# A decoder layer on one core: the second feed-forward stage in two passes of seven block products

## What is computed

```python
def swiglu(h, wg, wu, wd):
    return (jax.nn.silu(h @ wg) * (h @ wu)) @ wd

h = x * (1 + mod[:, 1]) + mod[:, 0]
x = layer_norm(ALPHA*x + 0.5*mod[:, 2]*swiglu(h, ffn1_wg, ffn1_wu, ffn1_wd), ...)
h = x * (1 + mod[:, 4]) + mod[:, 3]
out = mixer(h)                       # attention, then w_out
x = layer_norm(ALPHA*x + mod[:, 5]*out, ...)
h = x * (1 + mod[:, 7]) + mod[:, 6]
x = layer_norm(ALPHA*x + 0.5*mod[:, 8]*swiglu(h, ffn2_wg, ffn2_wu, ffn2_wd), ...)
```

## Time and profile before

| what | value |
|---|---|
| runs | 2271.41, 2273.47, 2273.75 us; median 2273.47 |
| profiled execution, first to last instruction | 2265.1 us |
| median less the profiled span | 8.4 us |
| mean granted TensorE clock, share of full | 0.986 |
| busy share of PE, DVE, ACT, POOL | 95%, 34%, 26%, 27% |

### The profile page before, as it was taken

One profiled execution on the slowest core, in us unless ns is written; L12 is line 12 of the kernel. 1 busy time (PEld: TensorE's weight loads), 2 busy tenths in 40 slices (PEclk: granted clock), 3 DMA queues, 4 the chain that ended last, 5 costly groups with the idle time before them and its releaser, 6 DMA issues.

```text
span 2265.1 us, 33136 instructions
## 1 busy us (share of the span) xinstructions
PE 2161.6 (95%) x13244; PEld 1976.8 (87%) x13244; DVE 778.9 (34%) x1709; ACT 580.7 (26%) x1071; POOL 614.4 (27%) x397
## 2 busy tenths in 40 slices
PE   6799999999999998999979989999999999999997
PEld 2689999999999997998844449899999999999995
DVE  1532122321223229202365652751222211222327
ACT  2311111112111123422265561361111111111114
POOL 1232322223222230124233333132323232323210
PEclk8899999999999999999989999999999999999999
DMA  8372222321321110413242012111111111111002
GB/s 288 131 231 94 84 66 93 112 93 38 112 93 38 47 38 19 148 47 108 101 169 106 1 38 66 38 47 48 56 37 56 37 56 37 56 37 56 28 1 75
DMA packets 168942, 171.36 MB, mean 76 GB/s; under 512 B 14370, under 2 KB 130834, under 8 KB 168324
## 3 DMA queue, kind: packets, MB, share of 16 engines
q1 hardware_dynamic: 168836, 169.84, 23.2%
HBM read 156.91 MB, written 19.20 MB: 78 GB/s over the span
## 4 chain that ended last, share of the span: by engine, by line
PE 87%; DVE 6%; ACT 2%; issue 2%; SPq 2%; DMA 1%; POOL 0%; DVEq 0%; ACTq 0%
PE psum L211 26%; PE psum L213 25%; PE psum L212 25%; PE psum L1086 2%; PE psum L546 2%; PE psum L1145 1%; PE psum L987 1%; DVE NT L694 1%; PE psum L1443 1%; DMA ADA<-in_w_ada 1%; SPq L499 1%; PE psum L644 1%; DVE Y L659 1%; DVE Y L679 1%; PE psum L1136 1%
## 5 line engine op out<-in xcount | busy, mean ns | idle before, releaser
L211 PE MATMUL psum<-Hhi,Whi 128*128 128x344 f32 x2736 | 878.7, 321 | 19.5 <-DVE Hlo L703 10.3
L213 PE MATMUL psum<-Hhi,Wlo 128*128 128x344 f32 x2736 | 875.2, 320 | 0.0
L212 PE MATMUL psum<-Hlo,Whi 128*128 128x344 f32 x2736 | 874.4, 320 | 0.0
L313 POOL TENSOR_TENSOR Wlo<-RAW,Whi 128x1024 fp32r<-128x1024 f32 x158 | 383.2, 2446 | 696.9 <-ACT Whi L309 696.3
L211 PEld LDWEIGHTS psum<-Hhi,Whi 128*128 128x128 f32 x2736 | 515.9, 189 | 29.9 <-issue 23.0
L213 PEld LDWEIGHTS psum<-Hhi,Wlo 128*128 128x128 f32 x2736 | 515.6, 188 | 0.0
L212 PEld LDWEIGHTS psum<-Hlo,Whi 128*128 128x128 f32 x2736 | 514.9, 188 | 0.3
L436 DVE TENSOR_TENSOR GF<-SIL,psum 128x344 f32<-128x344 f32 x132 | 67.6, 512 | 902.7 <-ACT SIL L400 900.1
L443 DVE SCALAR_TENSOR_TENSOR Y<-psum,G,Y 128x344 f32<-128x344 f32 (+1 forms) x528 | 301.2, 573 | 180.5 <-PE psum L213 180.5
L211 PE MATMUL psum<-Ghi,Whi 128*128 128x344 f32 x1056 | 340.2, 322 | 2.4 <-DVE Y L443 2.4
L212 PE MATMUL psum<-Glo,Whi 128*128 128x344 f32 x1056 | 338.0, 320 | 0.0
(11 more groups left out here) (192 smaller groups left out, 1312.0 us busy)
## 6 DMA issues: line engine op xcount, KB each, us to landing
ADA<-in_w_ada SPq DMA_DIRECT2D x38, 1024.0 KB, 9.6
RAW<-in_ffn_wg SPq DMA_DIRECT2D x44, 512.0 KB, 3.8
RAW<-in_ffn_wu SPq DMA_DIRECT2D x44, 512.0 KB, 3.7
RAW<-in_ffn_wd SPq DMA_DIRECT2D x44, 512.0 KB, 3.7
RAW<-in_w_in SPq DMA_DIRECT2D x36, 256.0 KB, 3.2
SK<-in_cache_a_k SPq DMA_DIRECT2D x24, 256.0 KB, 3.5
...
```

The source lines that it names most:

```text
L211: pe.matmul(out, whi, xhi, start=first, stop=False)
L212: pe.matmul(out, whi, xlo, start=False, stop=False)
L213: return pe.matmul(out, wlo, xhi, start=False, stop=last)
L313: pool.tensor_tensor(Wlo[slot][:, :, :], RAW[raw][:, :, :], Whi[slot][:, :, :].bitcast(F32), ALU.subtract).then_inc(W[phase].ready, 1)
```

## The change

The 1032 columns of the second feed-forward stage become four groups of 258 (GQ). A pass works on two groups side by side (pass 0: groups 0 and 1; pass 1: groups 2 and 3), and both passes go over all 11 chunks, so there are 22 chunk-passes and all weights are fetched and split twice. In a chunk-pass the gate and the up product are each a 2x2 block product: 2 tiles of D_FF by 2 halves of D_MODEL, times 2 halves of D_MODEL by 2 groups of columns. Instead of eight block products, seven are made, of sums and differences of blocks (the Winograd form of Strassen's method); each block product is 4 tiles times three matmuls of 258 columns. The sums of weights are made by VectorE (`row_sums`, `row_differences`), those of the inputs once a pass (`column_sums`), and results are combined in PSUM and by ScalarE and VectorE (`part_act`, `add_dve`). The low parts of the blocks stay on GpSimd (`row_lo`), the low parts of the down weights move to VectorE (`drow_lo`). The output projection also works in four groups of 258. The norm of groups 0 and 1 behind the stage, and the store of the first four blocks of 128 tokens, move into pass 1; five blocks are left for the end.

The core of the diff:

```diff
+GQ = T // 4
+NP = 7
...
+        LOWK, HIGHK = slice(0, KT // 2), slice(KT // 2, KT)
+        W_SOURCE = [[PAIR[u][:, 0, LOWK, :], PAIR[u][:, 0, HIGHK, :], S2[u][:, :, :], S1[u][:, :, :],
+                     PAIR[u][:, 1, LOWK, :], PAIR[u][:, 0, HIGHK, :], PAIR[u][:, 1, HIGHK, :]] for u in range(2)]
+        W_SUM = {2: 3, 3: 1, 4: 5, 5: 7}
...
+        def row_sums(dve, r, first=False):
+            for u in range(2):
+                if u == 0 and not first:
+                    dve.wait_ge(r_ready, PR * r - 6)
+                dve.wait_ge(pair_in[u], 32 * r + 32)
+                dve.tensor_tensor(S1[u][:, :, :], PAIR[u][:, 1, LOWK, :], PAIR[u][:, 1, HIGHK, :], ALU.add).then_inc(sums_done, 1)
+            for u in range(2):
+                dve.wait_ge(sums_done, 8 * r + 1 + u)
+                dve.tensor_tensor(S2[u][:, :, :], S1[u][:, :, :], PAIR[u][:, 0, LOWK, :], ALU.subtract).then_inc(sums_done, 1)
...
+        def product_pe(pe, r, n, p, fresh=False, first=False):
+            i, u = n // 2, n % 2
+            a, x = bank[2 * u], bank[2 * u + 1]
+            pe.wait_ge(r_ready, PR * r + n + 1)
...
+            out = (x if i in (1, 3, 5) else a)[:, 0:GQ]
+            whi, wlo = Rhi[n % NP], Rlo[n % NP]
+            for k in range(KT // 2):
+                pe.matmul(out, whi[:, k, :], Thi[i][:, k, :], start=(k == 0 and i in (0, 1, 3)), stop=False, skip_group_check=True)
+                pe.matmul(out, whi[:, k, :], Tlo[i][:, k, :], start=False, stop=False, skip_group_check=True)
+                last = pe.matmul(out, wlo[:, k, :], Thi[i][:, k, :], start=False, stop=(k == KT // 2 - 1), skip_group_check=True)
+            last.then_inc(prod_done, 1)
+        def down_pe2(pe, r, v, first=False):
+            side, d = 1 - v // KT, v % KT
+            if v == 0:
+                pe.wait_ge(dw_ready, 2 * r + 2)
+            if v % KT == 0:
+                pe.wait_ge(g_ready2, 4 * r + 3 + v // KT)
+            if v >= 3:
+                pe.wait_ge(y_evac2, ROWS2 * r + v - 2)
+            elif not first:
+                pe.wait_ge(y_evac2, ROWS2 * r)
+            bk = bank[4 + v % 3][:, 0:GQ]
+            for j in range(2):
+                last = mm3(pe, bk, Whi[4 + j][:, d, :], Wlo[4 + j][:, d, :],
+                           Ghalf[0][:, j, side, :], Ghalf[1][:, j, side, :], j == 0, j == 1)
+            last.then_inc(down_done2, 1)
+        def chunk_pe(pe, r, p, fresh=False, first=False, mean=None, early=None, last=False):
+            for n in range(PR):
+                product_pe(pe, r, n, p, fresh, first)
+                if n == 3 and mean is not None:
+                    for g in mean:
+                        mean_pe(pe, *g)
+                if early is not None and n in (3, 9):
+                    early_turn_pe(pe, early, n // 6)
+            if first:
+                pe.wait_ge(ln_centered, ln[2].n_at(3))
+            for v in range(ROWS2):
+                down_pe2(pe, r, v, first)
+                if last and v == ROWS2 - 2:
+                    mean_pe(pe, ln[3], 3)
...
+        def later_blocks(dve, r):
+            add_dve(dve, r, 1, 0)
+            add_dve(dve, r, 1, 1)
+            gf_dve2(dve, r, 1)
+            for j in range(2):
+                drow_lo(dve, r, j)
+            add_dve(dve, r, 2, 0)
+            add_dve(dve, r, 2, 1)
+            gf_dve2(dve, r, 2)
+            gf_dve2(dve, r, 3)
+        def downs_dve(dve, r, p, more=True, norm=None):
+            for v in range(KT):
+                down_dve2(dve, r, p, v, norm)
+            if more:
+                row_sums(dve, r + 1)
+            elif p:
+                dve.wait_ge(y_evac2, ROWS2 * r + KT)
+                samples_in(dve, ln[3])
+            for v in range(KT, ROWS2):
+                down_dve2(dve, r, p, v, norm)
+        def chunk_dve(dve, r, p, center_at=None, scale_at=None):
+            row_differences(dve, r)
+            if scale_at is not None:
+                scaled(dve, *scale_at)
+            first_blocks(dve, r)
+            if center_at is not None:
+                center(dve, *center_at)
+            later_blocks(dve, r)
+            downs_dve(dve, r, p)
...
+        def chunk_pool(pool, r, more=True):
+            for n in range(NP, PR):
+                row_lo(pool, r, n)
+            g_lo_pool2(pool, r, 0)
+            for b in range(1, 4):
+                g_lo_pool2(pool, r, b)
+            if more:
+                for n in range(NP):
+                    row_lo(pool, r + 1, n)
```

More of the change, by code:

```diff
@@ new lines, in inputs_dve @@
+        def inputs_dve(dve, g):
+            n, p, side = ln[2], g // 2, g % 2
+            own = n.prompt(g)
+            m = own.stop - own.start
+            dve.wait_ge(ln_scaled, n.scaled_at(g, 1))
+            if m < GQ:
+                ts = NQ[side][:, :, m:]
+                step_dve(dve, dve.tensor_tensor(ts, Y[:, :, TP:], A9[:, :, 1:], ALU.mult))
+                dve.tensor_tensor(ts, ts, B9[:, :, 1:], ALU.add)
+            for k in range(KT):
+                last = dve.tensor_scalar(NQ[side][:, k, 0:m], Y[:, k, own], A9[:, k, 0:1], B9[:, k, 0:1], ALU.mult, ALU.add)
+                if side == 0 and k == KT // 2 - 1:
+                    last.then_inc(t_src, 1)
+            last.then_inc(t_src, 1)
@@ new lines, in column_lo, with residual_pool @@
+        def column_lo(dve, p, i):
+            dve.wait_ge(t_hi, NP * p + i + 1)
+            dve.tensor_tensor(Tlo[i][:, :, :], T_SOURCE[i], Thi[i][:, :, :].bitcast(F32), ALU.subtract).then_inc(t_ready, 1)
+        def residual_pool(pool, g):
+            pool.wait_ge(t_src, (2, 3)[g])
+            for k in range(KT):
+                y = Y[:, k, ln[2].cols(g)]
+                last = pool.tensor_scalar(y, y, yv[:, 0, k:k + 1], yv[:, 1, k:k + 1], ALU.mult, ALU.add)
+            last.then_inc(res_done, 1)
@@ L1832, in _ @@
+            chunk_act(act, CH + 2, std_at=(ln[3], 0))
+            input_hi(act, ln[3], 0)
+            for b in range(4):
+                chunk_act(act, CH + 3 + b, early=b)
+            with act.Fori(CH + 7, 2 * CH - 1) as c:
+                chunk_act(act, c)
+            chunk_act(act, 2 * CH - 1, more=False)
+            square(act, ln[3], 3)
             load_sqrt(act)
-            square(act, ln[3], 1)
-            std(act, ln[3], 0)
-            input_hi(act, ln[3], 0)
-            std(act, ln[3], 1)
@@ new lines, in _ @@
+            row_differences(dve, 0)
+            first_blocks(dve, 0)
+            column_lo(dve, 0, 3)
+            last_column_sum(dve, 0)
+            for i in range(4, NP):
+                column_lo(dve, 0, i)
+            later_blocks(dve, 0)
+            center(dve, ln[2], 2)
+            center(dve, ln[2], 3)
+            prep_gate(dve, 8, 0.5)
+            dve.wait_ge(res_done, 2)
+            downs_dve(dve, 0, 0)
+            chunk_dve(dve, 1, 0, scale_at=(ln[2], 2))
+            chunk_dve(dve, 2, 0, scale_at=(ln[2], 3))
@@ new lines, in _ @@
+            inputs_dve(dve, 2)
+            chunk_dve(dve, 3, 0)
+            inputs_dve(dve, 3)
+            chunk_dve(dve, 4, 0)
+            column_sums(dve, 1)
+            with dve.Fori(5, CH - 1) as c:
+                chunk_dve(dve, c, 0)
+            row_differences(dve, CH - 1)
+            first_blocks(dve, CH - 1)
+            column_lo(dve, 1, 0)
+            column_lo(dve, 1, 1)
+            column_lo(dve, 1, 2)
+            add_dve(dve, CH - 1, 1, 0)
+            add_dve(dve, CH - 1, 1, 1)
@@ new lines, in _ @@
+            gf_dve2(dve, CH - 1, 1)
+            for j in range(2):
+                drow_lo(dve, CH - 1, j)
+            column_lo(dve, 1, 3)
+            last_column_sum(dve, 1)
+            add_dve(dve, CH - 1, 2, 0)
+            add_dve(dve, CH - 1, 2, 1)
+            gf_dve2(dve, CH - 1, 2)
+            column_lo(dve, 1, 4)
+            gf_dve2(dve, CH - 1, 3)
+            downs_dve(dve, CH - 1, 0, norm=ln[3])
+            for i in range(5, NP):
+                column_lo(dve, 1, i)
+            dve.wait_ge(res_done, 4)
@@ new lines, in _ @@
+            prep(dve, None, None, 2, last_norm=True)
+            chunk_dve(dve, CH, 1, center_at=(ln[3], 1))
+            chunk_dve(dve, CH + 1, 1, scale_at=(ln[3], 1), center_at=(ln[3], 0))
+            chunk_dve(dve, CH + 2, 1, scale_at=(ln[3], 0))
+            for b in range(4):
+                chunk_dve(dve, CH + 3 + b, 1)
+            with dve.Fori(CH + 7, 2 * CH - 1) as c:
+                chunk_dve(dve, c, 1)
+            row_differences(dve, 2 * CH - 1)
+            first_blocks(dve, 2 * CH - 1)
@@ new lines, in _ @@
+            chunk_pe(pe, CH + 2, 1)
+            pe.wait_ge(ln_hi, ln[3].k_at(0, KT - 1))
+            for b in range(4):
+                chunk_pe(pe, CH + 3 + b, 1, early=b)
+            with pe.Fori(CH + 7, 2 * CH - 1) as c:
+                chunk_pe(pe, c, 1)
+            pe.wait_ge(early_act, 8)
+            chunk_pe(pe, 2 * CH - 1, 1, last=True)
+            mean_pe(pe, ln[3], 2)
+            var_pe(pe, ln[3], 3)
+            var_pe(pe, ln[3], 2)
```

(6 more changed lines are left out.)

637 lines of the change are left out of this document (447 added, 190 removed).

## The result

The changed kernel takes 2315.19 us (median of four runs, 2313.24 to 2320.17) against 2273.61 for the kernel before (2271.41 to 2280.18). The ratio is 1.0185, 95% interval 1.0163 to 1.0208: the change costs 41.6 us. I had forecast 2298.5, a cost of 25.

The account below looks back on a forecast made before the run. TensorE, busy 95%, was taken as the bound. Its work -40, steady loss +44, start +18, change of pass +5, norm in pass 1 +15 and end -15 gave +27, taken as +25: 2298.5 us, range 2250 to 2325.

Parts of the forecast that it names:

- The range: Whole kernel: 2250 to 2325 us; by the matmul interval alone, 2283 at 0.1178 and 2325 at 0.1286.
- The interval: TensorE's time per 258-column matmul: 0.1213 us, assuming 0.014 is lost once a matmul.
- the rival: TensorE's matmuls: the interval grows with the columns, 0.1178 us at 258, giving 2283 us; chance 0.15.
- TensorE's work: Matmuls alone: 32.0 us a chunk-pass, -42.6 over 11 chunks, +2.7 in the output projection; together -40 us.
- The steady loss: Each steady chunk-pass: 2.1 us lost above 32.0, giving 34.1; 21 times, +44 us.
- the split of G: Before the first down product: TensorE sees block 2 at 20.6, products end at 20.4, so 0.2 us lost.
- The start: First chunk-pass with the norm ahead: 44 us over a plain one against 25.7 before, +18 us.
- The change of pass: Last chunk-pass of pass 0: block 2's split at 24.8 instead of 20.4, `two_sums` add 0.7; +5 us.
- The last chunk-pass and the end: After the last down product: 30 us of norm, turns and store against 45.0 before, -15 us.
- The sum itself: Whole kernel: terms give +27, taken as +25; span 2290 plus 8.4 us outside it gives 2298.5.
- sums covered: Steady chunk-passes: the ring of banks covers the row sums, loss 0.2, time 2258 us; chance 0.25.
- The rival of contention: VectorE and GpSimd on SBUF: waits worse than one, 2 us more a chunk-pass, 2340 us; chance 0.08.

Follow-up runs that it names:

- Run 2: Changed kernel with the first `drow_lo` of each chunk-pass moved ahead of the second add of block 1; 2323.25 us, ratio 1.0225.
- Run 10: Changed kernel with sums spread, first three down products begun with block 1, centrings earlier and GpSimd's residual updates partly behind `row_lo` 7 and 8; 2282.93 us.
- run 9: Changed kernel with sums behind down products 5, 7, 9, 11 and the first three down products begun with block 1 of G; 2293.38 us, ratio 1.0092.
- run 1: Changed kernel with the four row sums behind down products 5, 7, 9 and 11, one each, instead of all behind 7; 2299.21 us, ratio 1.0123.

## Why the prediction was right in direction and short in size

The sum of the prediction against the trace, in us from the last matmul of the projection:

| stage | forecast | measured | difference |
|---|---|---|---|
| to the start of chunk-pass 1 | 74.5 | 82.8 | +8.3 |
| chunk-passes 1 to 5 | 5 * 34.1 + 3.5 = 174.0 | 180.7 | +6.7 |
| 6 to 9 | 136.4 | 135.7 | -0.7 |
| 10 (change of pass) | 39.1 | 42.7 | +3.6 |
| 11 to 17 (norm and turns) | 7 * 34.1 + 15 = 253.7 | 256.1 | +2.4 |
| 18 to 20 | 102.3 | 102.0 | -0.3 |
| 21 and the end | 32.0 + 30.0 = 62.0 | 64.9 | +2.9 |

- **The range** holds the measured time, but partly by luck: its upper end, 2325, is that of an interval of 0.1286, which no row shows. Its two values by the interval also leave out the projection's 768 matmuls, which move them to about 2280 and 2330.
- **The interval** was near: 0.120 in the products and 0.119 in the down products, 0.1213 forecast. Over one column a cycle at 2.4 GHz 0.0125 and 0.0115 are left, where 344 columns left 0.014. Lost once a matmul it would still be 0.014, and in proportion to the columns 0.0105. The 264 matmuls of a chunk-pass, 31.6 us, lie halfway between my 32.0 and the rival's 31.1, so they do not decide between the two.
- **TensorE's work** was right in the projection, +2.7 as forecast (94.5 against 91.8), where the rival gives nothing. In a chunk-pass it was 0.4 too high.
- **The steady loss** was right in sum, by luck, and wrong in its parts. I had 2.1 us: 0.2 at the first down product, 1.55 at product 11 and 0.35 for the shared access. It is 33.9 - 31.6 = 2.3: 0.85 at the first down product and 1.47 at product 11 (each with 0.1 in the interval behind the hole, 0.22 us), and no wait of the sums. The step that failed is the split of G. I had the adds of block 2 done at 18.6 us after the start of product 0, and TensorE with G at 20.6, 0.2 behind the products' end at 20.4. The second `drow_lo` meets GpSimd and takes 1.67 us in place of 1.22, the adds are done at 18.9 and G is there at 20.9, while the products end at 20.15: 0.75 late. That lateness in turn lets GpSimd end `row_lo` 3 (1805.95) as the sums begin (1805.90), which removes the 0.35. Run 2 shows the link: take the first wait away, and the second comes back.
- **The start** is the largest miss of one step. I costed VectorE's chain and left out the first work that GpSimd has there, the 16 residual updates. They hold `row_lo` 7 until 1492.7, and product 7 waits for it. The centrings of groups 2 and 3 cost their 5.7 us on top, which I had. Moving either one alone brought 0.9 and 1.3 us. The granted clock of 0.81 over this stage is part of the miss. Run 10 recovers 7.2 of the 8.3 us, with the two edits on top of run 9.
- **Chunk-passes 1 to 5** were taken as plain, but for one variance. Numbers 3 to 5 have the inputs and sums of groups 2 and 3 on VectorE and the residual on ScalarE. With these the hole at the first down product is 1.9 to 2.2 us wide from start to start, and twice the clock falls behind it (0.95 in two of these rows):

```profile
1601.56:1636.55 34.99, 32.14 (x267) 31.71 (x266) 24.47 (x44) 17.37 (x37) 22.07 (x18) 1.00 0.31 90
1636.55:1673.26 36.71, 33.68 (x267) 33.25 (x265) 25.22 (x46) 18.40 (x40) 21.46 (x18) 0.95 0.30 86
1673.26:1710.77 37.51, 33.97 (x267) 33.32 (x266) 25.85 (x39) 15.49 (x33) 21.62 (x18) 0.95 0.29 84
```

- **The change of pass** was priced as 4.4 us of delay and 0.7 of pair sums; it costs 8.8. VectorE has 32.1 us of work in 42.7, but in the wrong place: TensorE waits 5.2 us for `Ghalf` and 2.4 for evacuations.
- **The last chunk-pass and the end** are 34.2 and 30.7 us, where I had 32.0 and 30.0. In number 21 I had counted TensorE's matmuls alone, but two holes of 0.73 and 0.83 us from start to start stay, and four matmuls of the mean of group 3 stand ahead of its last down product. In the end the root of group 3 comes 11.1 us after the last down product, not 10.1; part of its variance runs at the lower clock, 0.43 us a matmul.
- **The sum itself** forgot 2.5 us in the other direction: the last chunk before took 70.4, not 67.9. And the median lies 3.0 us above the profiled span after the change, where I took 8.4. That was a wrong reading: each run of the changed kernel is 1.8 us longer than the span recorded for it, so of the 8.4 about 6.6 were only that a fast execution had been profiled. The profiled span was forecast at 2290 and is 2312.2, 22 us short; the median is 16.7 short.

Of the rivals, "sums covered" was wrong as a forecast (2258) and right about its mechanism: the place of `row_sums` decides, and run 1 shows 1.45 us a chunk-pass for it. The rival of contention was the nearest to what happened when something was moved. The rule of the Trainium skill (TensorE: Matmul & The Clock Gate, "Back-to-back issue gap") gives an estimate of 0.110 for 258 columns; the trace has 0.120 and does not agree.

What stays open: I have not shown what each engine costs at the edges, beyond the waits read there and the two edits of the start, nor how much of the start is the clock alone, since nothing here holds the clock and keeps the holes. Nor does any run separate the two passes from the seven products: none makes the two-pass form without the sums of columns.
